# Projection units spread through each attention step of a two-layer transformer kernel

## The chip, the core and the metric

The kernel runs on one core of a Trainium2 chip. Five engines work side by side: TensorE (PE) for matrix products, VectorE (DVE), ScalarE (ACT) and GpSimd (POOL) for elementwise work, and SyncE (SP), which here issues the loads of the weights. Each engine works through its own list of instructions in order and waits on semaphores for the others. The metric is the device time of one execution in microseconds (us).

## What is computed

Input is one sequence of 256 tokens, 1024 wide. The first block has a modulated RMS norm, a projection, a block attention (MoBA, 8 heads of 64; with 256 tokens it is one causal block), an RWKV-7 time mix beside it, gates, an output projection, and a mixture of experts over 16384 experts (PEER). The second block has a retention layer and then a multi-head latent attention layer (MLA, 16 heads, keys of 128 + 64, values of 128). The parts that matter here:

```python
# MoBA, one block: per head
s_own = einsum(q, k) * 64 ** -0.5 ; causal mask
p = softmax(s_own) ; o = p @ v
...
g_moba, g_rwkv = split(sigmoid(gate_logits), 2)          # projection in_g
mixed = g_moba * (o_moba @ w_proj_moba) + g_rwkv * (o_rwkv @ w_proj_rwkv)

# MLA, per head
sc = (einsum(q_nope, k_nope) + einsum(q_rope, k_rope)) * 192 ** -0.5 ; causal mask
o = softmax(sc) @ v
return (o * silu(gate)) @ w_out                          # q: projection uqn, gate: projection b_g
```

## The kernel before

Everything is held transposed (features on the 128 partitions, tokens along the free dimension). A projection streams its weights from memory in chunks of up to 1 MB. Each float32 weight and each activation is split into a high and a low part that PE can multiply quickly: ACT makes the high part of a weight chunk (`hi`, L1098, two halves), DVE the low part (`lo`, L1625, two halves), or POOL for some tensors, `in_g` among them (L2304). A product is then three matmuls (high by high, high by low, low by high). Only two split chunks fit at once (`NS = 2`), so the high part of chunk n + 1 waits until PE has used up chunk n - 1. It is issued when chunk n is begun.

A **unit** of a projection is one `yield` of `proj_steps`: half the depth of a chunk for one of its two tiles of 128 output features. That is 9 matmuls of 256 columns in `uqn` (depth 768) and 12 in `in_g` and `b_g` (depth 1024). A chunk has four units. The finished pair of tiles is read from PSUM by ACT (a copy, L1108 in `uqn`; a tanh in the gates, L1298 and L1546), and in `b_g` DVE then multiplies it on.

Both attentions run as a loop of **steps** with such units beside them. Step i of PE has `scores(i)` (L481, into PSUM), `turned(i - 2)` (three transpositions of the softmax weights, L609) and `values(i - 3)` (weights by values), and then the units: two in MoBA, three in MLA. ACT's step i has the two exponentials of head i with their sums (L1090, from `ar, small`), the copy of the transposed weights of head i - 2 (128x384) and the copy of the values of head i - 3 (128x256 or 64x256), and then its part of the units. DVE's step i has the end of the softmax of head i - 2 (a reciprocal L1617, multiplications L1685 and L1686), then the scaling and masking of head i's scores (L1609) and their two maxima (L1676, L1677), and then its part of the units. In the last MLA steps DVE also gates two finished heads at a time and makes their low part (`gated`, `heads_rest`), and ACT their high part (`heads_out`).

The order is written out by hand. Each engine's program is a set of Python generators; `some(steps, n)` takes n units of the side work, and all engines walk the same sequence of chunks. So where a `yield` stands in a generator sets where a unit stands on that engine. Weight loads go through SP in the order of the chunks, each when the low part of the chunk that held its slot is done. `in_g` gives 16 of its 32 units to MoBA. In MLA, 28 units of `uqn` and 28 of `b_g` stand beside 19 steps.

Of the kernel before, what the change touches and what calls it, by code (L numbers as in the profile page):

```python
# [455 lines left out]
def tensor_program(q, m):  # L456
# [139 lines left out]
    def attention(tag, heads, dv, parts, vof, base, pts, scs, need):  # L596
        def scores(h):
            b = bank((tag, "sc", h))
            for x in need:
                p.wait_ge(*on(x))  # L600
            pr = parts(h)
            mm(b[:, 0:128], [(x[:, 0:128], k[:, 0:128]) for x, k in pr])
            mm(b[:, 128:384], [(x[:, 128:256], k[:, 0:256]) for x, k in pr]).then_inc(*p.up((tag, "sc", h)))

        def turned(h):
            b = bank((tag, "tr", h))
            p.wait_ge(*on((tag, "weights", h)))
            for i in range(3):
                ins = q.transpose(b[:, i * P:(i + 1) * P], scs[h % 3][:, i * P:(i + 1) * P], ident)  # L609
            ins.then_inc(*p.up((tag, "tr", h)))  # L610

        def values(h):
            b = bank((tag, "va", h))
            o = base(h)
            p.wait_ge(*on(("out", (tag, "tr", h))))
            mm(b[o:o + dv, 0:256], [(vof(h, 0), pts[h % 2][:, 0:256])], stop=False)
            mm(b[o:o + dv, 128:256], [(vof(h, 1), pts[h % 2][:, 256:384])], start=False).then_inc(*p.up((tag, "va", h)))

        for i in range(heads + 3):
            if i < heads:  # L620
                scores(i)
            if 2 <= i < heads + 2:
                turned(i - 2)
            if i >= 3:
                values(i - 3)
            yield
# [178 lines left out]
    def front():  # L805
# [36 lines left out]
        fill = beside_recurrence()  # L842
# [10 lines left out]
        for _ in norms():  # L853
# [1 line left out]
        at = attention("moba", 8, 64, lambda h: [(head(m.qk[:, 0:4, :], h), head(m.qk[:, 4:8, :], h))],  # L855
                       lambda h, kt: m.Vt[:, kt, 64 * h:64 * h + 64], lambda h: 64 * (h % 2), m.att1[1], m.att1[0],
                       ["qk ready"])
        for _ in at:
            some(gates, 2)
        finish(gates)  # L860
        ring["ids"] = list(range(7))
        proj("pr", 12, "ors")
# [177 lines left out]
    def mla():  # L1040
        proj("kvd", 0, by="xs4")
        proj("kvr", 0)
        colsum(("lat", "ms"), m.sq6, 4, ("lat", "squared"))
        rotB("kr", m.kr[:, 0:1, :], ("out", ("kvr", 0)))
        proj("b_q4", 0)
        proj("b_q2", 0)
        colsum(("ql", "ms"), m.sq6, 6, ("ql", "squared"))
        proj("kvk", 8, "lats")
        proj_tok("kvv", 8)
        finish(proj_steps("b_g", 0, js=(0,)))  # L1050
        steps = proj_steps("uqr", 8, by="qls")
        for f in range(0, 8, 2):
            some(steps, 4)
            if f > 0:
                rotB(("qr", f - 2), m.Qr[:, f - 2:f, :], ("out", ("uqr", f - 2)))
        finish(proj_steps("uqn", 8, js=(0,)))
        rotB(("qr", 6), m.Qr[:, 6:8, :], ("out", ("uqr", 6)))
        fill = chain(proj_steps("uqn", 8, js=range(1, 8), of=side), proj_steps("b_g", 0, js=range(1, 8), of=side))
        ring["ids"], ring["at"] = list(range(5)), 0

        def parts(h):
            lo = 64 * (h % 2)
            p.wait_ge(*on(("out", ("uqn", h - h % 2))))
            return [(m.Qn[:, h, :], m.Kn[:, h, :]), (m.Qr[lo:lo + 64, h // 2, :], m.kr[lo:lo + 64, 1, :])]

        for _ in attention("mla", 16, 128, parts, lambda h, kt: m.V3[:, kt, h * P:(h + 1) * P], lambda h: 0, m.att3[1],
                           m.att3[0], ["qr roped"]):
            some(fill, 3)
        finish(fill)
        ring["ids"], ring["at"] = list(range(7)), 0  # L1070
        with_sums("b_o", ("ln", 1), m.X, m.lnB, 8, "os2")
# [8 lines left out]
def scalar_program(q, m):  # L1080
# [72 lines left out]
    def attention(tag, heads, evac, pts, scs):  # L1153
# [17 lines left out]
        for i in range(heads + 3):  # L1171
            if i < heads:
                scores(i)
            if 2 <= i < heads + 2:
                turned(i - 2)
            if i >= 3:
                values(i - 3)
            yield
# [10 lines left out]
    def front():  # L1189
# [116 lines left out]
            AC(head(m.Om, h), b[64 * (h % 2):64 * (h % 2) + 64, 0:256], ACT.Copy, name)  # L1306

        for i, _ in enumerate(attention("moba", 8, evac, m.att1[1], m.att1[0])):
            some(gates, 2)
            if i == 3:  # L1310
                split_act("ors", m.Yy, 12, "o rwkv")
        finish(gates)
        a.mark("om")
# [212 lines left out]
    def mla():  # L1526
# [42 lines left out]

        at = attention("mla", 16, lambda h, b, name: AC(m.Qn[:, h, :], b[:, 0:256], ACT.Copy, name), m.att3[1], m.att3[0])  # L1570
        for i, _ in enumerate(at):
            some(fill, 3)
            if 11 <= i < 15:
                heads_out(i - 11)
        finish(fill)
        for i in range(4, 8):
            heads_out(i)
# [13 lines left out]
def vector_program(q, m):  # L1591
# [74 lines left out]
    def attention(tag, heads, scale, scs):  # L1666
# [21 lines left out]
        for i in range(heads + 3):  # L1688
            if 2 <= i < heads + 2:
                weights(i - 2)  # L1690
            if i < heads:
                scores(i)
            yield

    def barrier(n):
        v.mark(("all", n, "dve"))
# [3 lines left out]
    def front():  # L1700
# [105 lines left out]
        for _ in norms():  # L1806
            some(gates, 4)
        for i, _ in enumerate(attention("moba", 8, 0.125, m.att1[0])):
            some(gates, 2)
            if i == 3:  # L1810
                split_act("ors", m.Yy, 12)
        finish(gates)
        split_act("oms", m.Om, 8)
# [419 lines left out]
    def mla():  # L2233
# [38 lines left out]
                            ALU.subtract).then_inc(*v.up(("os2", "half", i // 4)))  # L2272

        for i, _ in enumerate(attention("mla", 16, float(192.0 ** -0.5), m.att3[0])):
            some(fill, 3)
            if i >= 11:
                gated(i - 11)
            if 12 <= i < 16:
                heads_rest(i - 12)
        finish(fill)  # L2280
        for i in range(4, 8):
            heads_rest(i)
# [267 lines left out]
```

## Time and profile before

| | us |
|---|---|
| median of 3 runs | 1947.89 (1947.28 to 1948.58) |
| the profiled execution | 1946.55 |
| its span in the trace | 1944.8 |
| PE busy | 1796.4, 92% of the span |
| DVE busy | 1139.5, 59% |
| ACT busy | 794.7, 41% |
| POOL busy | 205.2, 11% |

Busy time tells how much an engine has to do. Where an engine stands still, the trace names the instruction that released it. PE's busy time is modelled and says nothing of its clock: the granted clock of a stretch is given beside it, as a share of 2.4 GHz. MoBA's steps run from about 335 to 390 us, MLA's from about 1727 to 1876 us.

### The profile page before, as it was taken

How to read it: one execution, taken by the hardware profiler on the slowest of the kernel's cores; microseconds unless marked ns; L12 is line 12 of the kernel's file. 1: busy time of each engine (PE TensorE's matmuls, PEld its weight loads, DVE VectorE, ACT ScalarE, POOL GpSimd, SP SyncE). 2: the span in 40 equal slices, each digit the busy share in tenths (PEclk: the TensorE clock that was granted, in tenths of full speed). 3: DMA queues.
4: the chain of work that ended last, by engine and by line, in shares of the span. 5: the costliest groups of instructions: out<-in, count | busy, mean ns of one | idle time of the engine just before them, and what ended most of it. 6: DMA issues, size and time to landing. Idle time of an engine off the chain costs nothing.

```text
span 1944.8 us, 30066 instructions
## 1 busy us (share of the span) xinstructions
PE 1796.4 (92%) x13092; PEld 1644.0 (85%) x13092; DVE 1139.5 (59%) x1707; ACT 794.7 (41%) x1143; POOL 205.2 (11%) x84
## 2 busy tenths in 40 slices
PE   5879898898989999999999999999999998998887
PEld 3778787688989899998898888888899988987787
DVE  2373238465588838875436997555664646454554
ACT  2633314544434432234443323444444535534433
POOL 0030124200356720000000000000000000000000
PEclk8899989899989999999999999999999999989989
DMA  7233712234444443335554333554654343443220
GB/s 293 90 109 132 259 67 84 90 131 143 161 150 176 155 171 111 122 111 191 181 187 161 109 111 128 195 194 174 256 182 149 132 143 130 144 138 109 87 87 22
DMA packets 40022, 280.29 MB, mean 144 GB/s; under 512 B 4433, under 2 KB 4689, under 8 KB 7506
## 3 DMA queue, kind: packets, MB, share of 16 engines
q1 hardware_dynamic: 39024, 275.53, 39.7%
q10 hardware_dynamic: 866, 2.84, 0.4%
q8 instruction: 103, 1.69, 0.3%
q14 instruction: 29, 0.24, 0.0%
HBM read 277.30 MB, written 1.05 MB: 143 GB/s over the span
## 4 chain that ended last, share of the span: by engine, by line
PE 78%; DVE 14%; ACT 5%; POOL 2%; DMA 1%; issue 1%; ACTq 0%; DVEq 0%
PE ps L481 77%; DVE WL L1625 2%; ACT ar L1090 2%; POOL WL L2304 2%; DVE ar L1617 2%; ACT WH L1098 1%; DVE ar L1598 1%; DVE ar L2020 1%; DVE ar L1609 1%; DVE ar L2017 1%; DMA con<-in_con 1%; DVE ar L2024 1%; PE ps L609 0%; DVE ar L2036 0%; DMA ar<-in_in_qk 0%
## 5 line engine op out<-in xcount | busy, mean ns | idle before, releaser
L481 PE MATMUL ps<-RH,WH 128*128 128x256 f32 x2520 | 747.4, 297 | 49.9 <-DVE RL L1657 13.3
L481 PE MATMUL ps<-RL,WH 128*128 128x256 f32 x2520 | 729.0, 289 | 0.0
L481 PE MATMUL ps<-RH,WL 128*128 128x256 f32 x2520 | 727.9, 289 | 0.0
L1625 DVE TENSOR_TENSOR WL<-ar,WH 128x1024 fp32r<-128x1024 f32 (+1 forms) x398 | 467.8, 1207 | 384.5 <-ACT WH L1098 384.4
L1098 ACT ACTIVATE WH<-ar 128x1024 fp32r<-128x1024 f32 (+1 forms) x478 | 480.0, 1039 | 281.4 <-PE ps L481 266.7
L481 PEld LDWEIGHTS ps<-RH,WH 128*128 128x128 f32 x2520 | 500.0, 198 | 62.7 <-issue 16.7
L481 PEld LDWEIGHTS ps<-RL,WH 128*128 128x128 f32 x2520 | 500.2, 198 | 3.4 <-issue 2.9
L481 PEld LDWEIGHTS ps<-RH,WL 128*128 128x128 f32 x2520 | 499.4, 198 | 0.0
L481 PE MATMUL ps<-ar 128*128 128x64 f32 (+9 forms) x2988 | 340.5, 303 | 30.4 <-DMA con<-in_con 16.5
L481 PEld LDWEIGHTS ps<-ar 128*128 128x128 f32 (+6 forms) x2988 | 279.6, 172 | 69.8 <-issue 22.5
L481 PE MATMUL ps<-WH,RH 128*128 128x512 f32 (+1 forms) x704 | 262.5, 373 | 6.3 <-DVE RL L1998 6.3
L481 PE MATMUL ps<-WH,RL 128*128 128x512 f32 (+1 forms) x704 | 258.8, 368 | 0.0
L481 PE MATMUL ps<-WL,RH 128*128 128x512 f32 (+1 forms) x704 | 258.5, 367 | 0.0
L2304 POOL TENSOR_TENSOR WL<-ar,WH 128x1024 fp32r<-128x1024 f32 x80 | 205.0, 2586 | 496.2 <-ACT WH L1098 496.2
L481 PEld LDWEIGHTS ps<-WH,RH 128*128 128x128 f32 x704 | 133.6, 190 | 27.4 <-DVE RL L1998 6.7
L481 PEld LDWEIGHTS ps<-WH,RL 128*128 128x128 f32 x704 | 133.6, 190 | 22.0
L481 PEld LDWEIGHTS ps<-WL,RH 128*128 128x128 f32 x704 | 133.6, 190 | 20.3
L1404 ACT ACTIVATE ar<-ps 128x512 f32<-128x512 f32 x64 | 38.2, 597 | 274.5 <-PE ps L481 274.4
L1598 DVE TENSOR_TENSOR ar<-ps,ar 128x512 f32<-128x512 f32 (+3 forms) x72 | 47.1, 654 | 106.1 <-PE ps L481 89.2
L1974 DVE TENSOR_TENSOR ar<-con,ar 128x1024 f32<-128x1024 f32 x64 | 78.1, 1220 | 0.0
L481 PE MATMUL ps<-ar,con 128*128 128x256 f32 (+2 forms) x130 | 49.9, 507 | 13.0 <-DVE ar L1775 6.1
L1989 DVE TENSOR_TENSOR ar<-ar,ps 128x512 f32<-128x512 f32 x64 | 43.8, 685 | 29.7 <-PE ps L481 29.7
(134 smaller groups left out, 979.5 us busy)
## 6 DMA issues: line engine op xcount, KB each, us to landing
ar<-in_u SPq DMA_DIRECT2D x64, 1024.0 KB, 4.8
ar<-in_v SPq DMA_DIRECT2D x64, 1024.0 KB, 4.8
ar<-in_ada SPq DMA_DIRECT2D x24, 1024.0 KB, 4.9
ar<-in_in_g SPq DMA_DIRECT2D x8, 1024.0 KB, 4.8
ar<-in_wq SPq DMA_DIRECT2D x8, 1024.0 KB, 4.8
ar<-in_a_qk SPq DMA_DIRECT2D x8, 1024.0 KB, 10.6
ar<-in_a_v SPq DMA_DIRECT2D x8, 1024.0 KB, 4.8
ar<-in_a_g SPq DMA_DIRECT2D x8, 1024.0 KB, 4.8
```

What stands on the lines that cost most here:

```text
L481: ins = q.matmul(o, l, r, start=start and i == 0, stop=stop and i == len(pairs) - 1, skip_group_check=skip)
L1090: q.activation(o, x, f, **k).then_inc(*a.up(name))
L1098: q.activation(h[:, x:z, :], src[:, x:z, :], ACT.Copy).then_inc(*a.up(("hi", n, i)))
L1404: q.activation(m.H[:, i0:i0 + 2, :], tile(t).rearrange("p (n t) -> p n t", n=2), ACT.Gelu).then_inc(*a.up(("out", t)))
L1598: q.tensor_tensor(o, x, y, op).then_inc(*v.up(name))
L1609: q.scalar_tensor_tensor(o, x, s, y, op0, op1).then_inc(*v.up(name))
L1617: q.reciprocal(o, x).then_inc(*v.up(name))
L1625: q.tensor_tensor(l[:, x:z, :], src[:, x:z, :], h[:, x:z, :].bitcast(F32), ALU.subtract).then_inc(*v.up(("lo", n, i)))
L1974: q.tensor_tensor(m.rows_j[s], cst("iota").unsqueeze(1).broadcast_to([P, 8, P]), m.ids[:, 1, t:t + 8].unsqueeze(2).broadcast_to([P, 8, P]) ...
L1989: q.tensor_tensor(hv, hv, tile(b).rearrange("p (i t) -> p i t", t=8), ALU.mult).then_inc(*v.up(("gated", g, t)))
L2017: q.max(vals[:, s8], src).then_inc(*v.up())
L2304: q.tensor_tensor(l[:, x:z, :], src[:, x:z, :], h[:, x:z, :].bitcast(F32), ALU.subtract).then_inc(*g.up(("lo", n, i)))
```

## The change

The attention generators of all engines yield three times in a step instead of once, and each caller takes units at each of the three places: one each in MLA, and in MoBA one behind the scores and one behind the transposition. The number of units in a step stays the same. DVE's three yields stand together at the end of its step. What followed at the end of a given step (`split_act`, `heads_out`, `gated`, `heads_rest`) follows at the same step's third yield.

```diff
@@ tensor_program, attention; scalar_program, attention (the same lines)
             if i < heads:
                 scores(i)
+            yield
             if 2 <= i < heads + 2:
                 turned(i - 2)
+            yield
             if i >= 3:
                 values(i - 3)
             yield
@@ tensor_program, front
-        for _ in at:
-            some(gates, 2)
+        for i, _ in enumerate(at):
+            some(gates, i % 3 < 2)
@@ tensor_program, mla
-            some(fill, 3)
+            some(fill)
@@ scalar_program, front
-            some(gates, 2)
-            if i == 3:
+            some(gates, i % 3 < 2)
+            if i == 11:
                 split_act("ors", m.Yy, 12, "o rwkv")
@@ scalar_program, mla
-            some(fill, 3)
-            if 11 <= i < 15:
-                heads_out(i - 11)
+            some(fill)
+            if i % 3 == 2 and 11 <= i // 3 < 15:
+                heads_out(i // 3 - 11)
@@ vector_program, attention
             if i < heads:
                 scores(i)
+            yield
+            yield
             yield
@@ vector_program, front
-            some(gates, 2)
-            if i == 3:
+            some(gates, i % 3 < 2)
+            if i == 11:
                 split_act("ors", m.Yy, 12)
@@ vector_program, mla
-            some(fill, 3)
-            if i >= 11:
-                gated(i - 11)
-            if 12 <= i < 16:
-                heads_rest(i - 12)
+            some(fill)
+            if i % 3 == 2 and i // 3 >= 11:
+                gated(i // 3 - 11)
+                if i // 3 in range(12, 16):
+                    heads_rest(i // 3 - 12)
```

On PE, in an MLA step beside `uqn`, the order before is: the end of the units (`WH`, `WL` are the parts of the activations' and the weights' buffers as the trace names them), the scores (128x128 and 128x256 of `ar`), the transposition (L609), the values, the first products of the next units.

```order
9212 L481 MATMUL ps<-RL,WH 128x256
9213 L481 MATMUL ps<-RH,WL 128x256
9214 L481 MATMUL ps<-ar 128x128 x2
9215 L481 MATMUL ps<-ar 128x256 x2
9216 L609 MATMUL ps<-con,ar 128x128 x3
9217 L481 MATMUL ps<-ar 128x256
9218 L481 MATMUL ps<-ar 128x128
9219 L481 MATMUL ps<-RH,WH 128x256
```

The same step of PE in the changed kernel:

```order
9214 L481 MATMUL ps<-ar 128x128 x2
9215 L481 MATMUL ps<-ar 128x256 x2
9216 L481 MATMUL ps<-RH,WH 128x256
...
9224 L481 MATMUL ps<-RH,WL 128x256
9225 L609 MATMUL ps<-con,ar 128x128 x3
9226 L481 MATMUL ps<-RH,WH 128x256
...
9234 L481 MATMUL ps<-RH,WL 128x256
9235 L481 MATMUL ps<-ar 128x256
9236 L481 MATMUL ps<-ar 128x128
9237 L481 MATMUL ps<-RH,WH 128x256
```

Nine products moved between the scores and the transposition and nine between the transposition and the values; nine stay behind the values.

On ACT, in two MLA steps in a row, before. A chunk of weights is begun on the first unit in the one (high parts at row 589), and on the second unit in the other (row 595, behind the copy of the finished projection tile, L1108):

```order
585 L1090 ACTIVATE ar,small<-ar,small 128x128
586 L1090 ACTIVATE ar,small<-ar,small 128x256
587 L1090 ACTIVATE ar<-ps 128x384
588 L1090 ACTIVATE ar<-ps 128x256
589 L1098 ACTIVATE WH<-ar 128x768 x2
590 L1090 ACTIVATE ar,small<-ar,small 128x128
591 L1090 ACTIVATE ar,small<-ar,small 128x256
592 L1090 ACTIVATE ar<-ps 128x384
593 L1090 ACTIVATE ar<-ps 128x256
594 L1108 ACTIVATE ar<-ps 128x512
595 L1098 ACTIVATE WH<-ar 128x768 x2
```

The same two steps of ACT in the changed kernel, where the lines stand two lower (L1092 for L1090, L1100 for L1098, L1110 for L1108):

```order
585 L1092 ACTIVATE ar,small<-ar,small 128x128
586 L1092 ACTIVATE ar,small<-ar,small 128x256
587 L1100 ACTIVATE WH<-ar 128x768 x2
588 L1092 ACTIVATE ar<-ps 128x384
589 L1092 ACTIVATE ar<-ps 128x256
590 L1092 ACTIVATE ar,small<-ar,small 128x128
591 L1092 ACTIVATE ar,small<-ar,small 128x256
592 L1110 ACTIVATE ar<-ps 128x512
593 L1092 ACTIVATE ar<-ps 128x384
594 L1100 ACTIVATE WH<-ar 128x768 x2
595 L1092 ACTIVATE ar<-ps 128x256
```

In the first step the high parts moved ahead of both copies; in the second they and the projection tile's copy moved ahead of the values' copy. On DVE, POOL and SP the order of the instructions is that of before.

## Rows read from the trace of the kernel before

**Rows 1.** The page, part 4: shares of the chain that ended last.
```profile
PE 78%; DVE 14%; ACT 5%; POOL 2%; DMA 1%; issue 1%; ACTq 0%; DVEq 0%
```
**Rows 2.** PE's waits by releaser (total us, times, longest): 345:440, then 1700:1880.
```profile
PE ps L609 <- DVE ar L1686: 7.3, 3, 2.8
...
PE ps L609 <- DVE ar L1686: 19.6, 13, 3.5
```
**Rows 3.** Timeline (start, duration, engine, line, count, idle before), PE, an MLA step.
```profile
1756.77 2.05 PE L481 MATMUL ps<-ar 128*128 128x128 f32 x8
1758.75 0.55 PE L609 MATMUL ps<-con,ar 128*128 128x128 f32 x3
1759.13 0.82 PE L481 MATMUL ps<-ar 128*128 128x256 f32 x4
1759.71 0.36 PE L481 MATMUL ps<-RH,WH 128*128 128x256 f32 x1
1759.91 0.27 PE L481 MATMUL ps<-RL,WH 128*128 128x256 f32 x1
...
1763.01 2.05 PE L481 MATMUL ps<-ar 128*128 128x128 f32 x8
```
**Rows 4.** Timeline of DVE and ACT, the same MLA step.
```profile
1758.86 0.56 DVE L1609 SCALAR_TENSOR_TENSOR ar<-ps,con 128x384 f32<-128x384 f32 x1 [4.32 <-PE ps L481]
1761.32 0.96 ACT L1090 ACTIVATE ar<-ps 128x384 f32<-128x384 f32 x2
1762.18 1.57 ACT L1098 ACTIVATE WH<-ar 128x768 fp32r<-128x768 f32 x2
1764.91 0.17 DVE L1617 RECIPROCAL small<-small 128x2 f32<-128x2 f32 x1
```
**Rows 5.** Timeline of DVE, ACT and PE, the MLA step behind it.
```profile
1765.76 0.56 DVE L1609 SCALAR_TENSOR_TENSOR ar<-ps,con 128x384 f32<-128x384 f32 x1
1769.56 1.58 ACT L1098 ACTIVATE WH<-ar 128x768 fp32r<-128x768 f32 x2
1770.44 1.83 DVE L1625 TENSOR_TENSOR WL<-ar,WH 128x768 fp32r<-128x768 f32 x2 [3.48 <-ACT WH L1098]
1773.20 0.30 PE L609 MATMUL ps<-con,ar 128*128 128x128 f32 x1 [1.10 <-DVE ar L1686]
```
**Rows 6.** Timeline of PE, DVE and ACT, the last MLA steps.
```profile
1829.15 0.52 PE L609 MATMUL ps<-con,ar 128*128 128x128 f32 x3 [1.62 <-DVE ar L1686]
1847.37 0.69 DVE L1609 SCALAR_TENSOR_TENSOR ar<-ar 128x512 f32<-128x512 f32 x1
1849.59 0.52 PE L609 MATMUL ps<-con,ar 128*128 128x128 f32 x3 [2.90 <-DVE ar L1686]
1856.62 0.60 ACT L1546 ACTIVATE ar<-ps 128x512 f32<-128x512 f32 x1 [3.65 <-PE ps L481]
1860.11 0.55 PE L609 MATMUL ps<-con,ar 128*128 128x128 f32 x3 [3.52 <-DVE ar L1686]
```
**Rows 7.** Windows: length, busy time of each engine, then granted clock, DMA share, GB/s.
```profile
1749.00:1821.00 72.00, 62.74 (x421) 52.79 (x420) 34.99 (x77) 33.91 (x77) 0.00 (x0) 1.00 0.29 103
1829.00:1836.00 7.00, 6.85 (x44) 6.83 (x45) 3.16 (x7) 4.46 (x9) 0.00 (x0) 0.76 0.28 116
1850.00:1857.00 7.00, 6.58 (x41) 6.33 (x40) 0.71 (x3) 2.35 (x7) 0.00 (x0) 0.76 0.22 89
...
360.00:370.00 10.00, 8.53 (x46) 6.78 (x47) 4.79 (x15) 4.45 (x10) 3.90 (x2) 0.83 0.00 0
```
**Rows 8.** Timeline of PE in MoBA; last, a weight load of PE in MLA.
```profile
347.51 0.58 PE L481 MATMUL ps<-RH,WH 128*128 128x256 f32 x1 [1.41 <-POOL WL L2304]
...
361.48 0.55 PE L609 MATMUL ps<-con,ar 128*128 128x128 f32 x3 [2.83 <-DVE ar L1686]
...
381.29 0.52 PE L609 MATMUL ps<-con,ar 128*128 128x128 f32 x3 [2.68 <-DVE ar L1686]
...
1758.75 0.31 PEld L609 LDWEIGHTS ps<-con,ar 128*128 128x128 f32 x3 [0.33 <-issue]
```

## What was predicted

> **What bounds the kernel now.** I read the page's first and fourth part first. The chain that ended last runs over TensorE (PE) for 78% of the span [rows 1], so whatever PE waits for in a stage counts in full there, unless a later stage swallows it. Then the waits of PE by releaser, in the two stages that the change touches: in the MoBA attention the transpositions (L609) wait three times, 7.3 us in all, for VectorE's (DVE's) L1686, and in the MLA attention thirteen times, 19.6 us [rows 2]. L1686 is the second of the two multiplications that finish the softmax weights of a head. Nearly nothing else makes PE wait there. So 26.9 us of 1944.8 are the most that this reordering can take out of waits; what the clock does after them comes on top.
>
> Why are the weights late, when their exponential was done two steps before? The timeline of one MLA step shows it. PE's own work of a step without a wait is: scores at 1756.77, transposition at 1758.75, values at 1759.13, first product of the projection at 1759.71, next scores at 1763.01 [rows 3]. That is 1.98 + 0.38 + 0.58 + 3.30 = 6.24 us; 27 products are three units of 9, so a unit is 1.10 us, and one of 12 products (the gate projection) 1.47 us. Beside it DVE and ScalarE (ACT) run a ring that does not pass through PE: DVE's scaling of the scores, ACT's exponentials, ACT's copies of one transposition and one value tile, then ACT's two high parts of a weight chunk, DVE's two low parts, and only then DVE's next softmax weights. With D for the start of DVE's scaling: in the step of 1758.86 ACT's copies start at D + 2.46, the high parts at D + 3.32, the reciprocal at D + 6.05 [rows 4]. In the step of 1765.76 a projection tile is copied too: high parts at D + 3.80, low parts from D + 4.68 for 1.83, and PE's next transposition starts at D + 7.44, after a wait of 1.10 [rows 5]. 7.4 against 6.24 is that wait. A chunk has four units and a step three, so a chunk begins in three steps of four: on the first unit, the second, the third, then none. The step without a beginning has no low parts in it, DVE catches up, and PE does not wait.
>
> **The change part by part.** No instruction is added or removed. DVE, GpSimd (POOL) and the queue of weight loads (SP) issue the same instructions in the same order; only PE's and ACT's orders move.
>
> *PE.* One unit now stands between the scores and the transposition, one between the transposition and the values. The transposition is asked for one unit later relative to the scores, 1.10 or 1.47 us. Slack of one unit does not only shorten each wait: the ring may fall behind PE by a unit before PE stands still, and it catches up in the fourth step.
>
> *ACT.* Where a chunk begins on the first unit, its high parts now stand directly behind the exponentials, ahead of both copies: 0.86 earlier (D + 2.46 for D + 3.32) [rows 4]. On the second unit only the value copy goes behind them, about 0.4 earlier. On the third nothing gets ahead, and the value copy there waits for values that PE now makes two units later: with units of 1.47 at scores + 1.98 + 1.47 + 0.38 + 1.47 + 0.58, which is 5.9 us after the scores began, some 3.9 us after D. ACT reaches that copy at about D + 3.5, so up to 0.4 is lost and nothing won.
>
> *Re-entry.* After a small float32 group the second product of the projection starts 0.20 after the first, not 0.12 [rows 3]: 0.08 each time PE comes back to it. A step now comes back three times. What going from the projection straight to a transposition costs is not in this trace. From below the bound is nothing (the scores follow the last product with no gap to be seen); below nothing is excluded, since the same products run. From above it is the 0.33 us that the weight load of the transposition stands behind the scores [rows 8]. I take 0.05 per unit in all, near the 0.08 row, because that 0.33 has the last long float32 product of the scores in front of it, and such a product needs the array itself.
>
> *MLA summed.* I carry the rows forward from step 2, whose transposition is the first, with two rules: a transposition starts at the later of (scores + 1.98 + one unit) and (reciprocal + 0.90); D at the later of (scores + 2.09) and (reciprocal + 0.86). The ring lengths up to the reciprocal are 5.2, 6.15 and 6.6 in uqn chunks (old 6.05, 6.54, 6.6), and with the gates' chunks some 0.8 more, as their halves have 1024 columns for 768 and both conversions grow by that third (1.83 and half of 1.58 in [rows 5]). From step 12 on 1.33 more come in, for a gating and a low part that DVE does behind the chunk (1847.37 to 1849.59 in [rows 6], less the 0.90 behind the reciprocal). The scores then start at 1747.0, 1754.5, 1760.8, 1767.2, 1773.5, 1780.6, 1787.0, 1794.0, 1801.4, 1809.5, 1816.9, 1824.7 (steps 3 to 14; old: 1756.77 for step 4 and 1763.01 for step 5). Waits that stay: about 1.0 each before transpositions 1, 5 and 9, 0.4 before 11, then 1.8 and 2.3 before 12 and 13, because from step 12 on the ring (some 9 us) is longer than PE's step (7.4) in each of three steps. Before transposition 14 the old wait was 3.52: there are no scores any more and DVE first waits for ACT's gate copy at 1856.62 [rows 6]. With a unit in between 2.1 stays. Transposition 14 starts at 1848.0, not 1860.11 [rows 6]. From there the old order has 0.38 + 0.58 + 4.4 with 1.6 for the low clock, the same again without it, and 0.6 + 2.9 to the end of the last unit of the gates: 1875.9. The new one has three units and the two small groups, then 1.5 + 0.4 + 0.5 + 3.0 + 3.0: 1860.3. That is 15.6 us. Behind it the output projection's second half waits for DVE's last low parts. That chain starts at the same last unit; the values of head 15 now stand behind it on PE, so I leave the wait as it is.
>
> *The clock.* In 1829 to 1836, after a wait of 1.62, the granted clock is 0.76 on average, part of the time at the lower of its two levels (1.2 for 2.4 GHz): a quarter of 7 us, 1.7 us, is lost [rows 6, 7]. The same happens in 1850 to 1857 behind the wait of 2.90. Over 1749 to 1821, with eight waits of 0.7 to 1.5, it is 1.00 [rows 7]. The three long ones (1.62, 2.90, 3.52) become 0.4 to 2.3. I let two of the new ones still lower the clock, at 1.3 net each: 15.6 - 2.6 = 13 us.
>
> *MoBA summed.* Units are 12 products, two in a step. Transposition 2 waits 2.83 at 361.48 and transposition 5 waits 2.68 at 381.29 [rows 8]. The first stands behind a low part of another tensor that now begins 0.3 to 0.5 later: gain 1.5 - 0.4 = 1.1. The second stands behind the low parts of chunk pr 0, whose high parts now come 0.9 earlier, with 1.5 of unit: 2.4. Behind both the clock dropped (0.83 over 360 to 370, 1.7 us [rows 7]); I count half of it, 1.7 for both. On the other side the third of the waits, 1.8, for the first transposition, is no gain: the unit now ahead of it waits for POOL until 347.51 anyway [rows 8], and the transposition, which used that time, comes onto the path for 0.4. MoBA: 1.1 + 2.4 + 1.7 - 0.4 = 4.8, say 5.
>
> Together 18 us. The profiled execution took 1946.55 us, with a span of 1944.8; 1946.55 - 18 = 1928.5. The median is 1.3 us above that execution, so I say **1930**.
>
> **What the skill would make of it.** The clock's fall stands behind PE's long waits in the rows above. The Trainium skill ("TensorE: Matmul & The Clock Gate", Part 1) says that the throttled state is the default and that activity releases it. The trace agrees. By that rule alone none of the shortened waits would lower the clock, and the sum would be 18 + 2.6 + 1.7, 22 us. The rule that speaks against the change is on the same page (Part 2, step by step): only weight loads are pulled ahead, matmuls stay in program order, so a transposition that is ready cannot pass a unit that waits. The step at 347.51 is the one place here where that bites.
>
> **The rivals.**
> 1. *The clock stays up everywhere* once the waits are short: 18 + 2.6 + 1.7 = 22 us, 1926. For it: no drop behind eight waits of up to 1.5 [rows 7]. Against: waits of about 2 stay late in MLA. Chance 0.15.
> 2. *The ring sets the pace all the same.* If PE cannot run ahead of the ring (another tile's wait takes the place of L1686), only what ACT's order shortens is won: 3 x 0.86 + 4 x 0.4 in MLA, one unit before transposition 14, and 3 in MoBA: 8.7 us, 1939. For it: DVE's order is untouched, and every step with a chunk shows the ring longer than PE's work. Against: PE's rows leave one unit of room and the fourth step catches up. Chance 0.17.
> 3. *The wait was free.* The whole gain is taken back at the output projection or by a later load: 1948. Against: the DMA engines are busy for 0.2 to 0.3 in these windows [rows 7], and each later stage starts from PE's progress. Chance 0.05.
> 4. *Crossings cost more than the waits.* There are 38 more returns to the projection (two in each of 16 MLA steps, one in each of 6 MoBA steps). If each pair of crossings costs the 0.33 of [rows 8] both ways, that is 38 x 0.66 = 25 us, of which 2 are counted: 1930 + 23 = 1953. It makes the kernel slower from about 0.55 us per pair, since 20 us of gain stand against it. Against: 0.08 in the step without a wait [rows 3]. Chance 0.05.
>
> **How the numbers follow.** My forecast, 1930, has 0.58, with its own range 1926 to 1935. The range 1922 to 1939.5 takes in the first rival and the second down to its price. Faster by over 0.2% (3.9 us, about what a measurement of this kernel can tell from no change): 0.58 + 0.15 + 0.15 of the second rival = 0.88. Within 0.2%: 0.07. Slower: 0.05.
>
> **What would show it.** In the profile after: L609 waits for L1686 some 8 to 10 us in all instead of 26.9, with the longest left in the last quarter of MLA and two of about 1 beside uqn. The high parts (L1098, then L1100) start at D + 2.5 in steps whose chunk begins on the first unit. From the first MLA scores to the end of the last gate unit about 13 us are missing, in MoBA about 5. The mean granted clock of the last quarter of MLA rises. I am wrong if the waits of L609 stay above 15 us (rival 2), if the same waits come up under other names on the projection's first products, or if 12 products between two small groups take over 1.9 us at full clock (rival 4).

## The result, and the profile after

| | us |
|---|---|
| before, beside it (4 runs) | 1948.24 (1947.28 to 1949.32) |
| changed (4 runs) | 1918.76 (1915.12 to 1924.4) |
| ratio | 0.9851, 95% interval 0.9826 to 0.9876 |
| the profiled execution after, and its span | 1917.7, 1915.9 |

The changed kernel is faster by 1.5%, some 29 us, where 18 were forecast; its median lies below the range. From the page after, a line of part 1 and the chain's shares:

```profile
PE 1781.4 (93%) x13092; PEld 1631.8 (85%) x13092; DVE 1144.5 (60%) x1707; ACT 793.8 (41%) x1143; POOL 206.1 (11%) x84
...
PE 78%; DVE 13%; ACT 5%; POOL 2%; DMA 2%; issue 1%; ACTq 0%; DVEq 0%
```

The chain is as before [rows 1], with a point less for DVE. PE's waits for the second softmax multiplication (L1686 before, L1690 now) over the whole span, then over 1700 to 1880 (total us, times, longest):

```profile
PE ps L609 <- DVE ar L1690: 8.4, 7, 2.1
...
PE ps L609 <- DVE ar L1690: 7.4, 6, 2.1
```

That is 8.4 us for the 26.9 of [rows 2], within the forecast 8 to 10. The reordering does what it says. An MLA step of PE after, in the columns of [rows 3], whose step took 6.24 us:

```profile
1741.95 2.05 PE L481 MATMUL ps<-ar 128*128 128x128 f32 x8
1743.94 0.38 PE L481 MATMUL ps<-RH,WH 128*128 128x256 f32 x1
...
1745.10 0.49 PE L609 MATMUL ps<-con,ar 128*128 128x128 f32 x3
1745.35 0.36 PE L481 MATMUL ps<-RH,WH 128*128 128x256 f32 x1
...
1746.51 0.81 PE L481 MATMUL ps<-ar 128*128 128x256 f32 x4
1747.08 0.36 PE L481 MATMUL ps<-RH,WH 128*128 128x256 f32 x1
...
1748.23 0.38 PE L481 MATMUL ps<-ar 128*128 128x128 f32 x2
```

The scores start 6.28 us apart: two more crossings between projection and attention cost 0.04 us together. DVE and ACT in that step, as in [rows 4]:

```profile
1744.04 0.56 DVE L1613 SCALAR_TENSOR_TENSOR ar<-ps,con 128x384 f32<-128x384 f32 x1 [3.23 <-PE ps L481]
1746.32 1.56 ACT L1100 ACTIVATE WH<-ar 128x768 fp32r<-128x768 f32 x2
1747.98 0.97 ACT L1092 ACTIVATE ar<-ps 128x384 f32<-128x384 f32 x2
1749.05 0.17 DVE L1621 RECIPROCAL small<-small 128x2 f32<-128x2 f32 x1
```

The high parts stand ahead of both copies, at D + 2.28 (D is the start of DVE's scaling), and the reciprocal at D + 5.01, where [rows 4] had 3.32 and 6.05. The chunks that begin on the second and third unit have it at D + 6.06 and D + 6.54. The longest waits that stay, on PE:

```profile
339.12 0.58 PE L481 MATMUL ps<-RH,WH 128*128 128x256 f32 x1 [4.05 <-POOL WL L2310]
...
1825.80 0.87 PE L609 MATMUL ps<-con,ar 128*128 128x128 f32 x3 [1.93 <-DVE ar L1690]
...
1834.89 0.33 PE L609 MATMUL ps<-con,ar 128*128 128x128 f32 x1 [2.09 <-DVE ar L1690]
```

Where the time went, by stages cut at the same instructions in every trace: the start of the first MoBA scores, MoBA (to ACT's high part of its output), MLA (from the first scaling to the last gate tile's tanh), and what lies between and behind. "Clock loss" is worked out from windows of 2 us: length times (1 - granted clock), summed. (The expectations of the four runs with one attention or one engine alone measure MLA from its first scores to the end of its last unit instead: 148.7 us in before, 133.7 in after. Where a figure by that measure is given, it is called that.)

| | first MoBA scores at | MoBA | between | MLA | behind | clock loss in MoBA / MLA |
|---|---|---|---|---|---|---|
| before | 334.7 | 56.4 | 1340.1 | 145.0 | 68.6 | 6.8 / 8.6 |
| after | 326.3 | 49.6 | 1341.8 | 131.0 | 67.2 | 3.4 / 6.6 |

Of the 28.9 us between the two spans, 14.0 are MLA (forecast: 13), 6.8 MoBA (5), 1.4 what is behind (0), minus 1.7 between. The other 8.4 are in the front, where both kernels run the same instructions in the same order. So this pair of profiles looks like a small miss in the two stages and a gift from elsewhere. The experiments say that this is not how to read it.

### The profile page after: what moved, and what is told of

Same layout as the page of the kernel before. It is cut to its first block, busy times and chain, and to the rows that moved or that the text cites. A ratio compares the mean times of both kernels' runs of the same rounds, so it can differ in the third digit from the quotient of the medians.

```text
span 1915.9 us, 30068 instructions
## 1 busy us (share of the span) xinstructions
PE 1781.4 (93%) x13092; PEld 1631.8 (85%) x13092; DVE 1144.5 (60%) x1707; ACT 793.8 (41%) x1143; POOL 206.1 (11%) x84
## 3 DMA queue, kind: packets, MB, share of 16 engines
HBM read 277.30 MB, written 1.05 MB: 145 GB/s over the span
## 4 chain that ended last, share of the span: by engine, by line
PE 78%; DVE 13%; ACT 5%; POOL 2%; DMA 2%; issue 1%; ACTq 0%; DVEq 0%
PE ps L481 77%; DVE WL L1629 2%; POOL WL L2310 2%; ACT ar L1092 2%; DVE ar L1621 2%; ACT WH L1100 1%; DVE ar L1602 1%; DVE ar L2026 1%; DVE ar L2023 1%; DVE ar L1613 1%; DMA con<-in_con 1%; DVE ar L2030 1%; PE ps L609 0%; DVE ar L2042 0%; DMA ar<-in_in_qk 0%
## 5 line engine op out<-in xcount | busy, mean ns | idle before, releaser
L1100 ACT ACTIVATE WH<-ar 128x1024 fp32r<-128x1024 f32 (+1 forms) x478 | 480.0, 1039 | 283.3 <-PE ps L481 269.1
L481 PEld LDWEIGHTS ps<-RH,WH 128*128 128x128 f32 x2520 | 493.8, 196 | 71.1 <-issue 21.5
L481 PEld LDWEIGHTS ps<-RL,WH 128*128 128x128 f32 x2520 | 494.2, 196 | 3.4 <-issue 2.9
L481 PEld LDWEIGHTS ps<-RH,WL 128*128 128x128 f32 x2520 | 493.3, 196 | 0.0
```

Of the source, the lines that this page charges most:

```text
L481: ins = q.matmul(o, l, r, start=start and i == 0, stop=stop and i == len(pairs) - 1, skip_group_check=skip)
L1100: q.activation(h[:, x:z, :], src[:, x:z, :], ACT.Copy).then_inc(*a.up(("hi", n, i)))
```

## The experiments

Rival theories for the surplus, once the result was there. **A**: the ring was shorter, or PE's room larger, than in the replay (a term of the sum). **B**: the MLA waits cost more than their length, because the clock falls behind them oftener than the one trace of before showed. **C**, the sharp form of B: the waits of about 1 us alone cost clock, and filling them with idle products makes the old order faster although PE then does more. **D**: the surplus is chance in the front. (The expectations of the first two runs use two of these letters otherwise: their A is "made inside the two attentions, the rest is chance", their B "the 8 us that after is ahead at MoBA's start belong to the changed program". The expectations of the two repeats call that second one "Rival D".)

All runs are compared with runs of the kernel before on the same chip. PE_LATE and ACT_LATE put the three yields of an attention back to the end of the step, on that engine (`scalar_program` has the same lines with ACT_LATE):

```diff
             if i < heads:
                 scores(i)
-            yield
+            if not (tag in PE_LATE):
+                yield
             if 2 <= i < heads + 2:
                 turned(i - 2)
-            yield
+            if not (tag in PE_LATE):
+                yield
             if i >= 3:
                 values(i - 3)
+            if (tag in PE_LATE):
+                yield
+                yield
             yield
```

**The change in one attention.** First in MLA alone, `PE_LATE = ACT_LATE = ('moba',)`:

> The change in the MLA attention alone; MoBA keeps its units at the step's end, on PE and ACT. Theory A (the gain is made inside the two attentions, by the ring and one unit of slack, and the rest of the 29 us is the clock's chance in stages that hold the same instructions): from the first MLA scores to the end of the last gate unit 133.5 us as in the changed kernel (148.5 before), MoBA from first scores to the first product of pr 56 as before, time 15 us under before. The first 330 us may take anything from 326 to 335, as they hold the same instructions. Theory B (the 8 us that the changed kernel's trace is ahead when MoBA begins belong to the changed program, by where its instructions lie or by something that comes back from the later stages): MoBA begins at 326 here too if MLA's part causes it, at 335 if MoBA's part does, and the time is 15 or 23 us under before.

Measured: 1924.4 us (1923.71 to 1926.71) against 1947.32; ratio 0.9883 (0.9865 to 0.9901), 22.9 us less. That is 8 us more than the 15 of the expectation's A, and MLA, by the expectation's measure, took 130.5 us for 133.5. MoBA began at 331.0, not at 326, so the lead in the front does not come with the change in MLA. Then in MoBA alone, `('mla',)`:

> The change in the MoBA attention alone. Theory A: MoBA takes 49 us (56 before, 49 in the changed kernel), MLA 148.5 as before, time 7 us under before, give or take what the clock does in the stages before. Theory B: MoBA begins at 326 as in the changed kernel, and the time is 15 us under before.

Measured: 1941.84 us (1935.51 to 1943.49), ratio 0.9961 (0.9946 to 0.9976), 5.5 us less. MoBA took 49.6 us and began at 327.2, but the time is far from the 15 us of the expectation's B. The two add up to 28.4, about what the whole gave (29 us in the first comparison, 27 in the one below). MoBA did what was forecast; the surplus is in MLA. The windows of the MLA stage (length, busy time of PE, weight loads, DVE, ACT and POOL, granted clock, DMA share, GB/s), of before, after and the change in MLA alone:

```profile
1731.00:1876.00 145.00, 125.41 (x822) 109.96 (x822) 71.39 (x141) 65.40 (x141) 0.00 (x0) 0.94 0.28 97
```
```profile
1718.00:1849.00 131.00, 123.57 (x819) 107.74 (x819) 71.04 (x141) 64.66 (x141) 0.00 (x0) 0.95 0.31 108
```
```profile
1728.00:1855.00 127.00, 119.61 (x819) 103.89 (x819) 71.04 (x141) 64.62 (x141) 0.00 (x0) 0.99 0.32 111
```

The same MLA order takes 131 us at 0.95 in one trace and 127 at 0.99 in another. A single trace of a stage is not its length.

**Each kernel once more.** Before (no edit), and after (no edit):

> The kernel before, unchanged, for a second trace of it. Theory C (the clock's share was undersized: each wait of over about 1 us in MLA lowers the clock with some chance, and the trace of before that I read was a lucky one there): MLA from the first scaling to the last gate tile 147 to 150 us with 11 to 14 us of clock loss (145.0 and 8.6 in the first trace), and MoBA beginning at 327 to 332 rather than at 334.7. Rival D (the first trace was typical): 145 and 334.7 again, within 1, and the 8 us that the changed kernel is ahead at MoBA belong to the change.

> The changed kernel once more. Theory C: MLA 126 to 131 us with 2 to 7 us of clock loss, MoBA beginning anywhere from 326 to 332. Rival D: MoBA begins at 326 again.

Measured: before 1946.93 us (1942.45 to 1948.81, 10 runs), ratio 0.9999 (0.9984 to 1.0014); after 1920.56 us (1918.69 to 1921.09), ratio 0.9871 (0.9839 to 0.9903). So the change is worth 27 us here by the medians and 25 by the ratio, 29 in the first comparison. In these two traces MLA took 148.6 us with 14.0 lost to the clock and 127.9 with 3.0, and MoBA began at 331.6 and 331.8: all within what was expected of theory C, and against the rival by which MoBA begins at 334.7 and 326 again. The MLA stage of before again, and of after again:

```profile
1728.00:1877.00 149.00, 129.94 (x823) 113.74 (x823) 71.40 (x141) 65.17 (x141) 0.00 (x0) 0.91 0.27 95
```
```profile
1723.00:1851.00 128.00, 120.56 (x817) 104.67 (x817) 71.33 (x141) 64.36 (x140) 0.00 (x0) 0.98 0.32 109
```

The two traces of before hold nearly the same waits at the same places (the clock shifts a few: one of 1.62 us is gone in the second, the next is 2.17 for 1.28); what sets them apart is the clock. One such place: before, then before again, each time the transpositions with their waits and a window (of before: 1803 to 1815):

```profile
1802.79 0.52 PE L609 MATMUL ps<-con,ar 128*128 128x128 f32 x3 [1.14 <-DVE ar L1686]
1811.64 0.55 PE L609 MATMUL ps<-con,ar 128*128 128x128 f32 x3 [1.49 <-DVE ar L1686]
...
1803.00:1815.00 12.00, 10.52 (x78) 9.44 (x77) 5.85 (x12) 6.31 (x15) 0.00 (x0) 1.00 0.46 171
```
```profile
1800.47 0.87 PE L609 MATMUL ps<-con,ar 128*128 128x128 f32 x3 [1.14 <-DVE ar L1686]
1810.90 0.90 PE L609 MATMUL ps<-con,ar 128*128 128x128 f32 x3 [1.49 <-DVE ar L1686]
...
1800.00:1812.00 12.00, 10.05 (x55) 8.86 (x56) 6.28 (x14) 4.46 (x9) 0.00 (x0) 0.80 0.31 100
```

Waits of 1.14 and 1.49 in both. In one execution PE stays at 2.4 GHz; in the other it is at 1.2 for part of the stretch, the transposition takes 0.87 us for 0.52, and from it to the next one, with the same instructions between, it is 10.43 us for 8.85. Theory B holds, and with it a warning: the first trace of before had a lucky draw (8.6 us lost in MLA; three other traces with PE's old order there lost 14.0, 13.4 and 12.1: before again, the change in MoBA alone, and ACT's order alone, which is below).

**One engine's order alone.** PE's changed, ACT's as before, `ACT_LATE = ('moba', 'mla')`:

> Both attentions: PE in the changed order, ACT in the order of before (all units behind the copies). My prediction's arithmetic: the unit of slack on PE does most of it, the ring stays 0.86 longer in steps whose chunk begins on the first unit and 0.4 in those on the second: MLA 136 to 138 us instead of 133.5, MoBA 50 to 51, time 17 to 20 us under before. Rival (ACT's order is what counts, since the ring does not pass through PE): MLA 145, time 5 us under before.

Measured: 1935.29 us (1932.02 to 1937.95), ratio 0.9939 (0.992 to 0.9958), 12 us less, where 17 to 20 were expected. MLA took 137.8 us in its trace (141.5 by the expectation's measure, for 136 to 138) and MoBA 53.6 (for 50 to 51). Then ACT's alone, `PE_LATE = ('moba', 'mla')`:

> Both attentions: ACT in the changed order, PE in the order of before. My prediction's arithmetic: only the shortened ring is won, 0.86 in three steps and 0.4 in four, less some of the clock: MLA 144 to 145 us (148.5 before), MoBA 54 to 55, time 5 us under before. Rival (ACT's order counts): MLA 137, time 15 under before.

Measured: 1945.25 us (1942.54 to 1948.4, 10 runs), ratio 0.9991 (0.9979 to 1.0002): no difference that can be told; MLA 145.2 us (148.7 by the expectation's measure, for 144 to 145), MoBA 54.5 (for 54 to 55). So both MLA lengths, MoBA with PE's order alone, and both times came out longer than expected: each half alone is worth less than its share, 12 + 2 of 25 to 29. A reason stands in the timeline of DVE and ACT with PE's order alone:

```profile
1749.14 0.56 DVE L1627 SCALAR_TENSOR_TENSOR ar<-ps,con 128x384 f32<-128x384 f32 x1 [3.24 <-PE ps L485]
1751.61 0.49 ACT L1101 ACTIVATE ar<-ps 128x384 f32<-128x384 f32 x1
1752.46 0.38 ACT L1101 ACTIVATE ar<-ps 128x256 f32<-128x256 f32 x1 [0.36 <-PE ps L485]
1752.74 1.57 ACT L1109 ACTIVATE WH<-ar 128x768 fp32r<-128x768 f32 x2
```

ACT's value copy now waits 0.36 for values that PE makes two units later, and the high parts behind it start at D + 3.60 instead of D + 3.32 [rows 4]. The ring that ran beside PE has been led through PE. Left-over waits of L609 in MLA show the same: 13.5 us with PE's order alone and 17.4 with ACT's alone, for 19.6 [rows 2] with neither and 7.4 with both:

```profile
PE ps L609 <- DVE ar L1686: 19.0, 12, 3.5
```
```profile
PE ps L613 <- DVE ar L1704: 13.5, 11, 2.5
```
```profile
PE ps L613 <- DVE ar L1704: 17.4, 11, 3.5
```

(before again, PE's order alone, ACT's alone). The two orders must be moved together.

**Filling the waits (theory C).** The kernel before, with products of a matrix that is there anyway into an unused PSUM bank ahead of the MLA transpositions that wait: 8 as a rule, 16 and 24 before the two last of them, none in the steps that don't wait (4, 8 and 17), and none in step 2, whose wait of 1.0 stays. The results are read by nobody; the order of all else is that of before.

```diff
+FILLERS = {2: 0, 4: 0, 8: 0, 15: 16, 16: 24, 17: 0}
...
             b = bank((tag, "tr", h))
+            if tag == "mla":
+                for _ in range(FILLERS.get(h + 2, 8)):
+                    q.matmul(m.ps[7][:, 0:T], RH[:, 0, 0:P], RH[:, 1, :], start=True, stop=True)
             p.wait_ge(*on((tag, "weights", h)))
```

> The kernel before with idle work added: in MLA 8 more products of 256 columns, of no use to the result, in a bank that is free, stand before each transposition that waited in the trace of before (16 and 24 before the two longest waits, none in steps 4, 8 and 17). They fill PE's waits and shorten none of DVE's and ACT's ring. Theory C: the clock loss in MLA falls from 9 to 14 us to 0 to 4, and MLA comes out 5 to 9 us shorter than in the kernel before although it has more to do: 139 to 143 us, time 5 us under before. Rival (the waits alone were the cost, the clock follows something else): clock loss as before, MLA 147 to 151, time the same or up to 3 us over.

Measured: 1939.85 us (1935.32 to 1944.22, 10 runs) against 1947.55; ratio 0.9961 (0.9945 to 0.9977). Adding 120 idle products made the kernel 7.7 us faster. PE's waits and the window of MLA:

```profile
PE ps L615 <- DVE ar L1692: 5.4, 8, 1.0
...
1730.00:1872.00 142.00, 136.60 (x939) 120.11 (x939) 71.42 (x141) 65.33 (x141) 0.00 (x0) 0.97 0.28 98
```

MLA takes 142.4 us, against 146.8 on average in the three traces of the old order, and the clock loss falls from 12.0 to 3.6. Less than the 8.4 us of it come back, most likely because the fillers take PE's time where the ring was ready early. Nothing but the clock is seen that could make an unchanged order with more work shorter. The long waits were filled too, so this run alone does not say which waits cost clock. But the three longest cost 5.1 us of it in each trace of the old order (counted further down), so at least 3 of the 8.4 belong to waits of 0.7 to 1.5 us, and C holds. What is behind MLA also shrank, to 67.1 us from 68.6, though the order there and a wait of 1.8 us in it are those of before: by its clock, which lost 4.0 us there for 6.2 before.

**All units ahead of the transposition.** If slack is what counts, more of it should give more. Both engines take a step's units behind the scores, and transposition and values come last:

```diff
                 scores(i)
             yield
+            yield
+            if tag == "moba":
+                pass
+            else:
+                yield
             if 2 <= i < heads + 2:
                 turned(i - 2)
-            yield
             if i >= 3:
                 values(i - 3)
-            yield
+            if tag == "moba":
+                yield
```

> A step further than the change: all units of a step stand behind the scores, on PE and ACT, and the transposition and the values come last (three units of slack in MLA, two in MoBA). By the ring: ACT's high parts go ahead of both copies in every step, the ring is 0.9 shorter in all of them, and the waits of L609 (8.4 us in the changed kernel) fall to 0 to 3. MLA 122 to 126 us, MoBA 48 to 49, time 5 to 8 us under the changed kernel, 1911 to 1915. Rival: the remaining waits are the ring's last steps (gating, 9 us a step against PE's 7.4), which no slack of PE removes, or the copies that now stand last hold up the values: within 2 us of the changed kernel.

Measured: 1911.0 us (1910.79 to 1912.49), ratio 0.9826 (0.9794 to 0.9857), and 9.6 us less than the changed kernel had on the same chip. PE's waits over 1700 to 1880 name no transposition any more, and MLA takes 119.5 us, less than the 122 to 126 expected (MoBA 49.5, for 48 to 49):

```profile
PE ps L481 <- DVE ar L1612: 2.2, 1, 2.2
PE ps L481 <- DVE RL L2287: 1.2, 1, 1.2
...
1723.00:1842.00 119.00, 119.00 (x817) 104.64 (x817) 71.05 (x141) 64.46 (x140) 0.00 (x0) 0.98 0.34 120
```

The ring shortened too: with all high parts ahead of the copies, the reciprocal of a second-unit chunk comes at D + 5.48, where it had 6.06 in the changed kernel and 6.54 before.

**Filling what is left.** First that order, with 32 idle products ahead of the first unit of MoBA's third step, in the place of the 4.0 us wait for POOL; then the changed kernel with 8, 11, 15 and 16 idle products before MLA transpositions 1 and 12 to 14.

```diff
         for i, _ in enumerate(at):
+            if i == 6:
+                p.wait_ge(*on(("out", "ada rest")))
+                for _ in range(32):
+                    q.matmul(m.ps[7][:, 0:T], RH[:, 0, 0:P], RH[:, 1, :], start=True, stop=True)
             some(gates, i % 3 < 2)
```
```diff
+FILLERS = {3: 8, 14: 11, 15: 15, 16: 16}    # ahead of turned(h), by step h + 2; none elsewhere
```

> All units of a step behind the scores, as in the last run of the second call, and 32 idle products (256 columns, no use to the result, a free bank) where PE waits 4.0 us for POOL's low part in MoBA's third step. They end before that wait does, so they put nothing on the path at full clock. Theory C (a wait of PE lowers the clock behind it): the clock loss in MoBA falls from 3.4 us to under 1.7, MoBA takes 48 us or less (49.5), time 1 to 2 us under that run's 1911.0. Rival (what comes before MoBA has set the clock already, or the low part comes later than read): MoBA 49.5, same time.

> The changed kernel, with 8, 11, 15 and 16 idle products before the four transpositions of MLA that wait longest in it (steps 3, 14, 15, 16; 1.05, 1.46, 1.93 and 2.09 us). Theory C: clock loss in MLA 0 to 3 us (6.6, 2.2 and 3.0 in the three traces with this order), MLA 125 to 127 us, time 2 us under the changed kernel. If the clock loss in MLA stays spread over 2 to 7 us and MLA over 127 to 131, the waits that remain are not what sets it, and theory C holds only for the longer ones.

Measured, the first: 1908.42 us (1904.79 to 1909.24), ratio 0.98 (0.9782 to 0.9819). The fillers on PE, then MoBA's window without and with them:

```profile
340.46 4.09 PE L869 MATMUL ps<-RH 128*128 128x256 f32 x32
```

```profile
332.00:381.00 49.00, 43.11 (x283) 36.10 (x282) 30.91 (x58) 26.72 (x63) 15.38 (x7) 0.93 0.31 108
```
```profile
332.00:379.00 47.00, 45.09 (x315) 37.80 (x315) 31.41 (x58) 26.99 (x62) 16.02 (x7) 1.00 0.31 113
```

MoBA went from 49.5 to 47.3 us at full clock, though the fillers take as long (4.09 us) as the wait did. Its clock loss was 3.4 us in all five traces with the wait (after, after again, the change in MoBA alone, the kernel without these fillers, and the one below), and 0.0 here. By time the intervals of this kernel and the one without fillers overlap; the 2.2 us are shown by the traces alone. It is the fastest kernel of the study, 2.0% below before.

The second: 1919.12 us (1914.7 to 1922.74), ratio 0.9854 (0.9832 to 0.9876), the same as the change without fillers. Its MLA took 126.8 us with 2.1 lost to the clock, as good as any trace of that order, but its front fell badly, with the first MoBA scores at 337.4. Whether these fillers are worth their 1 to 2 us against an average MLA of 128.6 stays open: two of the three traces without them lost nothing behind those waits either (counted further down).

**The front.** Its instructions are the same in all twelve traces. The first MoBA scores of after and of the last kernel, with the window 0 to 325 of both:

```profile
326.32 0.92 PE L481 MATMUL ps<-ar 64*128 64x128 f32 x4
...
0.00:325.00 325.00, 271.10 (x2558) 228.24 (x2559) 141.76 (x179) 123.58 (x196) 60.82 (x29) 0.93 0.42 152
```
```profile
337.40 0.92 PE L484 MATMUL ps<-ar 64*128 64x128 f32 x4
...
0.00:325.00 325.00, 270.11 (x2476) 227.32 (x2477) 131.35 (x175) 116.59 (x188) 53.54 (x26) 0.88 0.41 149
```

Clock 0.93 against 0.88, 11.1 us apart. Theory D is right on the pair of profiles (8.4 of their 28.9 us) and wrong on the medians, which the change in MLA alone moved by 22.9.

## Why the prediction was right in sign and short in size

The averages over traces with the same MLA order (old: before, before again, the change in MoBA alone; new: after, after again, the change in MLA alone) put each term of the sum beside its measurement. MoBA goes by its own order (old: before, before again, the change in MLA alone, the fillers in MLA; new: after, after again, the change in MoBA alone).

| | forecast | measured |
|---|---|---|
| MLA without the clock | 15.6 - 6.5 = 9.1 | 134.8 - 124.7 = 10.1 |
| MLA, clock | 13 - 9.1 = 3.9 | 12.0 - 3.9 = 8.1 |
| MoBA, clock in it | 5 | 55.5 - 49.6 = 5.9 |
| behind MLA | 0 | 68.6 - 67.2 = 1.4 |
| sum | 18 | 25.5 |

(The 6.5 are the clock that the replay had within its 15.6: 1.6 behind each of three long waits, and 1.7 at 1744.6, where the 27 products behind the first transposition took 4.8 us in the trace and 3.3 in the replay.) The split is rough, since a slow stretch that ends ahead of a wait is partly taken up by it: before again lost 5.4 us more to the clock than before, and its MLA was 3.6 longer. Against 25.5 stand 25 to 27 and 29 us by time; what may be left, up to some 3 us, stays open between chance in the front and in the stretch between the attentions, which varied by 11 and by 6 us from trace to trace.

*PE and its crossings.* Right: 0.04 us in a step for 0.05 a unit. Rival 4, the only one on the slow side, is out, and with it the worry that a ready transposition stuck behind a unit would cost.

*ACT's order and the ring.* Right: high parts at D + 2.28 for D + 2.46, the ring 5.0, 6.1 and 6.5 to the reciprocal for 5.2, 6.15 and 6.6. Seen only in the runs of one engine alone: PE's new order without ACT's leads the ring through PE.

*Waits that stay.* Right where it mattered: 1.05 before transposition 1 (1.0), 1.46, 1.93 and 2.09 before 12, 13 and 14 (1.8, 2.3, 2.1). Too high before 5 and 9 (0.60 and 0.23 for 1.0) and 11 (none for 0.4): 7.4 us in all for 9.6. In the sum behind transposition 14, "three units and the two small groups" would give 1861.8; the 1860.3 goes with two units, as the rows have it. With no drop of the clock the change in MLA alone took 12.2 us there, for 12.3. Rival 2 (the ring sets the pace) is out; rival 3 too, since no stage behind took anything back.

*MoBA.* Right in the main: transposition 2 waits 0.99 at 353.39 (1.7 by the forecast), transposition 5 no more. The unit ahead of transposition 0 waits 4.05 for POOL and starts 12.80 us behind the first scores, as it did before. The clock gave 1.7 to 3.4 there, for 1.7.

*The clock in MLA.* This is the step that failed: "Over 1749 to 1821, with eight waits of 0.7 to 1.5, it is 1.00" [rows 7], and with it the term "15.6 - 2.6". The reading is right for its trace. But from that one trace I took it that waits of 1 to 1.5 us leave the clock alone, took the stage of before as that trace had it, and let two drops stay. What the clock lost in MLA (us), by windows cut at each drop; these sums lie 0.2 to 0.4 under those from windows of 2 us:

| | at the stage's start | behind waits under 1.6 | behind waits of 1.6 to 3.5 |
|---|---|---|---|
| before | 1.6 | 1.7 | 5.1 |
| before again | 1.9 | 6.8 | 5.1 |
| the change in MoBA alone | 2.8 | 5.1 | 5.1 |
| after | 2.8 | 0 | 3.4 |
| after again | 2.8 | 0 | 0 |
| the change in MLA alone | 1.8 | 0 | 0 |

The loss at the start stands behind a wait of 2.2 us that the first scores have in all twelve traces; no order of the attention changes it. In before, the start and the one short wait that cost clock are these:

```profile
1731.00:1755.00 24.00, 21.89 (x129) 18.92 (x129) 12.31 (x27) 10.36 (x25) 0.00 (x0) 0.86 0.34 119
...
1731.00:1744.00 13.00, 12.22 (x71) 10.27 (x70) 6.53 (x13) 5.61 (x13) 0.00 (x0) 0.87 0.23 82
1744.00:1748.00 4.00, 3.77 (x19) 3.77 (x20) 1.35 (x4) 1.59 (x5) 0.00 (x0) 0.58 0.76 262
```

So the trace that I had shows one such loss just ahead of the stretch that I quoted: 1.7 us, behind the wait of 1.02. Of the 27 waits of 0.7 to 1.5 in the three old traces (31 us in all) 8 cost 1.7 us each, 4.5 us a trace on average. The replay had 1.7 of that. The long waits cost 5.1 in each, as forecast (4.8).

The two drops that I let stay came in the trace of after, behind the waits of 1.93 and 2.09:

```profile
1825.00:1830.00 5.00, 4.20 (x21) 4.17 (x22) 1.79 (x6) 1.62 (x6) 0.00 (x0) 0.66 0.47 195
1835.00:1840.00 5.00, 5.00 (x29) 4.82 (x29) 3.51 (x6) 0.88 (x2) 0.00 (x0) 0.66 0.37 108
```

That is 1.7 us each, for 1.3. But the other two traces of that order have the same waits and no drop. The change in MLA alone:

```profile
1834.95 0.52 PE L613 MATMUL ps<-con,ar 128*128 128x128 f32 x3 [1.92 <-DVE ar L1704]
1842.50 0.55 PE L613 MATMUL ps<-con,ar 128*128 128x128 f32 x3 [2.09 <-DVE ar L1704]
...
1732.00:1855.00 123.00, 115.61 (x799) 99.89 (x799) 69.00 (x137) 62.05 (x135) 0.00 (x0) 1.00 0.33 115
```

So the new stage lost 1.1 us behind its waits on average, for 2.6, and was 2.2 shorter by waits that did not stay: 128.6 us, where 132 were forecast. The old stage took 146.8 on average, where the trace that I read has 145.0. Together they make the 18.2 us of MLA for 13. Rival 1 had the mechanism (the clock is given back where waits go), and in MLA it came true in two of three traces, but it took the size of the old loss from the same trace: 22 us, still 3 short.

Then the range: it had an end for each unknown cost, but took the stage of before as known. It is itself drawn anew in each execution (8.6 to 14.0 us lost in four traces).

## What to carry to other kernels

A wait on TensorE's path costs its length and, by chance, clock behind it (here 1.7 us behind 8 of 27 waits of 0.7 to 1.5 us), so add up (1 - granted clock) over the whole stage, not behind the longest waits alone, and treat that sum as one draw of many. Where a product group waits for a ring of other engines, put independent work ahead of it on TensorE, and on the engine that feeds the ring put the ring's instruction first: neither order alone gave half of what both gave. A wait that cannot be removed can be filled with idle products, which cost nothing while the wait lasts (32 of them in a wait of 4 us) and TensorE's time where it does not last as long as they do: with 120 of them MLA without its clock loss took 138.8 us for 134.8.

## What the hardware showed that I had not expected

The same waits (1.14 and 1.49 us) leave TensorE at 2.4 GHz in one execution, and in another each of them is followed by a stretch at 1.2; what makes the difference was not found out. The same holds for waits of 1.93 and 2.09 us (both in one trace of three, none in the others) and 2.15 and 2.17 (no drop in two traces), while the wait of 2.2 us at the start of MLA had a drop behind it in all twelve. With waits of 0.7 to 1.5 us all along, a stage of 145 to 149 us ran at a mean of 0.91 to 0.94; with 120 idle products in them at 0.97. The Trainium skill ("TensorE: Matmul & The Clock Gate", Part 1) says that the throttled state is the default and activity releases it. The trace agrees, with fillers that compute nothing as the activity. And the first 325 us, with the same instructions, ran at 0.88 to 0.93 and ended up to 11 us apart, which is why one pair of profiles cannot size a change of 1%.
